# Matrix products that take turns over PSUM banks: three loop orders changed in a one-core encoder block

## The chip, the core and the metric

The kernel runs on one core of one Trainium2 chip. The metric is the device time of one execution in microseconds (us). Before the change three runs took 2044.85, 2045.12 and 2049.2 us, median 2045.12. The engines are named as in the profile: PE is TensorE's products, PEld its weight loads, DVE is VectorE, ACT is ScalarE, POOL is GpSimd, SP is SyncE, which here issues DMAs.

## What is computed

One layer of an encoder block for 256 tokens of width 2048, in float32. Cut to what matters here:

```python
h = rms_norm(x, norm1_g)
z = h @ w_in                       # columns: attention q, k, v, gates; recurrence q, f, i, gate; two merge gates
ya = forgetting_attention(...) @ w_a_up
yb = gated_recurrence(...) @ w_b_up
x = x + (sigmoid(ga) * ya + sigmoid(gb) * yb) @ w_o
h2 = rms_norm(x, norm2_g)
q = h2 @ peer_wq                   # product keys: 16 of 128 x 128 experts for each token and head
x = x + sum over chosen experts of gate * gelu(h2 . U[expert]) * V[expert]
out = rms_norm(x, norm_f_g)
```

## The kernel before

Each float32 operand of a large product is split into a high and a low part of the type fp32r, and a product of two matrices is made of three: high by high, high by low, low by high, all added up in PSUM.

**Projections.** Weights come in 38 groups of 512 columns. A group is worked off in units of four 128-row blocks (`UK = 4`) of the contraction, four units to a group, or two where the contraction is 1024 long. For a unit SP loads 1 MB into `raw`, ACT writes its high part to `w_hi` (L606), DVE the low part to `w_lo` (L951), and PE waits once, for `lo_ready`, and then runs the unit's products into `acc`. `w_hi` and `w_lo` have two buffers each, so the next unit is split while PE works. `acc[128, 2, 1024]` is PSUM: group `g` uses the half `g % 2`, which is two banks of 512 float32 columns, and the other half is emptied meanwhile. The last product of a unit signals `unit_done`.

- A *transposed unit* (L1698 to L1701) has the weights stationary and 256 tokens moving. Its four feature blocks of 128 each take 256 columns: features 0 and 1 lie in the first bank, 2 and 3 in the second. There are 48 such units, of 4 x 4 x 3 = 48 products.
- A *natural unit* (L1715 to L1717) has a token tile of 128 stationary and 512 weight columns moving. Token tile 0 fills the first bank and tile 1 the second. There are 88 such units, of 4 x 2 x 3 = 24 products.

In both, the three products of one feature or one token tile follow each other.

**Middle.** The gather of expert rows and their dot products, and the scatter of the experts' weights, keep DVE, ACT, POOL and the DMA queues busy. PE has little to do there, and the change doesn't touch that code.

**Dense value stage.** The last 1344 columns of the value table are not gathered: for each of 128 blocks of 128 experts the whole block is loaded (`v_raw`, three buffers, SP), split by ACT into `v_hi` (L887) and by DVE into `v_lo` (L1637), and multiplied by the 128 x 128 weights of the block's experts (`e_hi`, `e_lo`) for each of two token tiles. One block for one token tile is a *pass* of nine products (L2021 to L2023): the 1344 columns are three pieces of 512, 512 and 320 (`VBANKS`), each in a bank of its own, in `acc` for token tile 0 and in `scr` for token tile 1, and each piece has three products. The last product of a pass signals `v_used`, on which ACT's and DVE's next write to these buffers waits. Beside this, POOL gathers the first 704 columns of the chosen rows (L560) and DVE adds them up (L1620).

What sets the order on PE is the program's text: each engine runs its own instructions as written, and semaphores hold them together. The loops of the three functions below are thus the order of the products.

Of the kernel before, what the change touches and what calls it, by code (L numbers as in the profile page):

```python
# [11 lines left out]
P = 128  # L12
S = 256
NT = S // P
# [4 lines left out]
GW = 512  # L19
FB = GW // P  # L20
# [12 lines left out]
UK = 4  # L33


def units_of(g):

    narrow = G_AUP <= g < G_GB or (G_GB <= g < G_WO and (g - G_GB) % 2)
    return (HW if narrow else D) // P // UK
# [17 lines left out]
BLOCKS = P  # L57
# [144 lines left out]
def build(nc, x, norm1_g, w_in, fox_f_bias, hg_lb_logits, hg_norm_g, w_a_up, w_b_up, w_o, norm2_g,  # L202
# [16 lines left out]
    with ctx:  # L219
# [26 lines left out]
        def at(name, kib, shape, dt=fp32):  # L246
            return nc.alloc_sbuf_tensor_at(name, [P, *shape], dt, offset=arena_at + int(kib * 1024))
# [5 lines left out]
        w_hi = at("w_hi", 64, [2, UK, GW], f32r)  # L253
        w_lo = at("w_lo", 80, [2, UK, GW], f32r)
# [22 lines left out]
        v_hi = at("v_hi", 184, [2, DW], f32r)  # L277
# [64 lines left out]
        acc = ctx.enter_context(nc.psum_tensor("acc", [P, 2, 2 * GW], fp32))  # L342
# [1326 lines left out]
        def _(pe):  # L1669
            t_ = nc.tensor  # L1670
# [12 lines left out]
            def transposed_unit(g, m, src, i=0, per=0):  # L1683

                pe.wait_ge(lo_ready, UNIT0[g] + m + 1 + i * per)
                if m == 0:

                    pe.wait_ge(acc_free[g % 2], 1 + g // 2 + i)
                hi_, lo_ = src
                end = m == units_of(g) - 1  # L1690
                for k in range(UK):
                    kk = m * UK + k
                    for f in range(FB):
                        to, cols = acc[:, g % 2, f * S:(f + 1) * S], slice(f * P, (f + 1) * P)
                        wh, wl = w_hi[:, m % 2, k, cols], w_lo[:, m % 2, k, cols]
                        last_k = end and k == UK - 1

                        t_.matmul(to, wh, hi_[:, kk, :], start=kk == 0 and f % 2 == 0, stop=False,  # L1698
                                  skip_group_check=True)
                        t_.matmul(to, wh, lo_[:, kk, :], start=False, stop=False, skip_group_check=True)  # L1700
                        last = t_.matmul(to, wl, hi_[:, kk, :], start=False, stop=last_k, skip_group_check=True)  # L1701
                last.then_inc(unit_done, 1)

            def natural_unit(g, m, src, i=0, per=0):

                pe.wait_ge(lo_ready, UNIT0[g] + m + 1 + i * per)
                if m == 0:
                    pe.wait_ge(acc_free[g % 2], 1 + g // 2 + i)
                hi_, lo_ = src
                end = m == units_of(g) - 1  # L1710
                for k in range(UK):
                    kk = m * UK + k
                    for t in range(NT):
                        to, cols = acc[:, g % 2, t * GW:(t + 1) * GW], slice(t * P, (t + 1) * P)
                        t_.matmul(to, hi_[:, kk, cols], w_hi[:, m % 2, k, :], start=kk == 0, stop=False)  # L1715
                        t_.matmul(to, hi_[:, kk, cols], w_lo[:, m % 2, k, :], start=False, stop=False)  # L1716
                        last = t_.matmul(to, lo_[:, kk, cols], w_hi[:, m % 2, k, :], start=False,  # L1717
                                         stop=end and k == UK - 1)
                last.then_inc(unit_done, 1)

# [25 lines left out]
            for n in range(4):  # L1746
                pe.wait_ge(normed, 2 + n // 2 * 2)
                transpose_norm(f"h{n}", n)
                if n:
                    pe.wait_ge(h_ready, n)  # L1750
                    transposed_unit(G_HQF, n - 1, hT)
            pe.wait_ge(h_ready, 4)
            transposed_unit(G_HQF, 3, hT)
            for g in range(G_HQF + 1, G_HIG):
                for m in range(4):
                    transposed_unit(g, m, hT)
            loop_two(G_HIG, natural_unit, hT)

            def level_products(name, a, b, side, pieces):
# [12 lines left out]
            for n in range(4):  # L1772
                g = G_FQK + n
                for m in range(4):
                    transposed_unit(g, m, hT)
                    if m % 2:
                        lv = 2 * n + m // 2
                        pe.wait_ge(level_ready, lv + 1)
                        e = level[lv % 2]
# [8 lines left out]
            to = scr[0:H, half, 0:S]  # L1788
            for k in range(KD):
                t_.matmul(to, wff_hi[:, k, :], hT_hi[:, k, :], start=k == 0, stop=False)  # L1790
                t_.matmul(to, wff_lo[:, k, :], hT_hi[:, k, :], start=False, stop=False)
                last = t_.matmul(to, wff_hi[:, k, :], hT_lo[:, k, :], start=False, stop=k == KD - 1)
            done("forget", last)

            natural_unit(G_FV, 0, hT)
            natural_unit(G_FV, 1, hT)
            natural_unit(G_FV, 2, hT)
            natural_unit(G_FV, 3, hT)
# [6 lines left out]
            for t in range(NT):  # L1805
                last = t_.transpose(scr[:, half, t * H:(t + 1) * H], ff[:, 1, t * P:(t + 1) * P], ident[0:H, 0:H])
# [56 lines left out]
            for n in range(4):  # L1863
                g = G_GA + n
# [26 lines left out]
            for n in range(4):  # L1891
                g = G_GB + 2 * n
                for m in range(4):
# [4 lines left out]
                    if n == 0 and m == 1:  # L1898
                        pe.wait_ge(ob_ready, 1)
                        for t in (1, 0):  # L1900
                            half = enter(f"ob{t}")
                            for h in range(H):
                                last = t_.transpose(scr[:, half, h * P:(h + 1) * P], o_hg[:, t, h * P:(h + 1) * P],
                                                    ident[:, :])
# [7 lines left out]
                if n < 2:  # L1912
                    pe.wait_ge(keys_in, 16)
                    half = enter(f"keys{n}")
                    for u in range(8):
                        last = t_.transpose(scr[:, half, u * P:(u + 1) * P], keys_sb[:, 8 * n + u, :], ident[:, :])
# [6 lines left out]
            for g in range(G_WO + 1, G_WQ):  # L1923
                for m in range(4):
                    natural_unit(g, m, hT)
                    if m == 2:
                        n = g - G_WO - 1
# [14 lines left out]
            for n in range(4):  # L1942
                g = G_WQ + n
# [67 lines left out]
            for n in range(BLOCKS):  # L2011
                e_cols = slice(n % 2 * P, (n % 2 + 1) * P)
                def add(t, pieces, low):

                    pe.wait_ge(e_ready, n // 2 * 2 + t + 1)
                    flat = (acc, scr)[t][:, :, :].rearrange("p a n -> p (a n)")
                    eh, el = e_hi[:, n // 2 % 2, t, e_cols], e_lo[:, n // 2 % 2, t, e_cols]
                    for at0, end in pieces:
                        to, cols = flat[:, at0:end], slice(at0, end)
                        stop = n == BLOCKS - 1  # L2020
                        t_.matmul(to, eh, v_hi[:, n % 2, cols], start=False, stop=False, skip_group_check=True)  # L2021
                        t_.matmul(to, eh, low[:, cols], start=False, stop=False, skip_group_check=True)  # L2022
                        last = t_.matmul(to, el, v_hi[:, n % 2, cols], start=False, stop=stop, skip_group_check=True)  # L2023
                    return last

                pe.wait_ge(v_ready, 2 * n + 2)
                for t in range(NT):
                    add(t, VBANKS, v_lo[n % 2]).then_inc(v_used, 1)
# [24 lines left out]
```

## Time and profile before

| | |
|---|---|
| median of three runs | 2045.12 us (2044.85 to 2049.2) |
| span of the profiled execution | 2047.2 us; the page gives no other time for it |
| PE busy | 1436.2 us, 70%, 7933 products |
| PEld busy | 1248.8 us, 7933 weight loads |
| DVE busy | 1608.7 us, 79% |
| ACT, POOL busy | 868.3 us, 42%; 994.3 us, 49% |
| mean granted PE clock | 0.841 of full |

The page cuts the span into 40 slices of about 51 us. Products on PE overlap: one lasts longer in the rows than the distance to the next one's start, and PE's throughput is read from the starts. PE's busy share is an average over stages that differ.

### The profile page before, as it was taken

How to read it: one execution, taken by the hardware profiler on the slowest of the kernel's cores; microseconds unless marked ns; L12 is line 12 of the kernel's file. 1: busy time of each engine (PE TensorE's matmuls, PEld its weight loads, DVE VectorE, ACT ScalarE, POOL GpSimd, SP SyncE). 2: the span in 40 equal slices, each digit the busy share in tenths (PEclk: the TensorE clock that was granted, in tenths of full speed). 3: DMA queues.
4: the chain of work that ended last, by engine and by line, in shares of the span. 5: the costliest groups of instructions: out<-in, count | busy, mean ns of one | idle time of the engine just before them, and what ended most of it. 6: DMA issues, size and time to landing. Idle time of an engine off the chain costs nothing.

```text
span 2047.2 us, 22565 instructions
## 1 busy us (share of the span) xinstructions
PE 1436.2 (70%) x7933; PEld 1248.8 (61%) x7933; DVE 1608.7 (79%) x1995; ACT 868.3 (42%) x1130; POOL 994.3 (49%) x699
## 2 busy tenths in 40 slices
PE   6999999999999999920000002212359999999997
PEld 6987998877888789920000001111247888888886
DVE  5465775454755556789999999977889999999998
ACT  4353443344343444311211226567856444444444
POOL 1002320000000000178888888888888788888862
PEclk9999999999999999965555555555569999999999
DMA  5555434444555555789999999999965999999996
GB/s 207 185 185 185 157 132 144 142 156 155 195 184 185 187 184 176 277 346 407 418 417 415 419 400 421 414 422 414 421 244 195 389 386 390 398 406 390 390 384 235
DMA packets 151803, 601.81 MB, mean 294 GB/s; under 512 B 14720, under 2 KB 14736, under 8 KB 118288
## 3 DMA queue, kind: packets, MB, share of 16 engines
q0 software_dynamic: 58048, 364.41, 44.0%
q1 hardware_dynamic: 93648, 236.02, 32.2%
q8 instruction: 61, 1.00, 0.2%
q14 instruction: 46, 0.38, 0.0%
HBM read 598.29 MB, written 2.10 MB: 293 GB/s over the span
## 4 chain that ended last, share of the span: by engine, by line
PE 55%; DVE 16%; issue 14%; POOL 7%; DMA 6%; ACT 2%; DVEq 0%; POOLq 0%; SPq 0%; ACTq 0%
PE acc L1715 7%; PE acc L1716 7%; PE acc L1717 7%; DVE slots L1470 6%; POOL slots L537 5%; PE acc L1698 4%; PE acc L1700 4%; PE acc L1701 4%; PE acc L2021 3%; PE scr L2022 3%; PE acc L2022 3%; DMA v_raw<-in_v_dense 3%; PE scr L2021 3%; PE scr L2023 3%; PE acc L2023 3%
## 5 line engine op out<-in xcount | busy, mean ns | idle before, releaser
L951 DVE TENSOR_TENSOR w_lo<-raw,w_hi 128x2048 fp32r<-128x2048 f32 x136 | 314.6, 2314 | 281.8 <-ACT w_hi L606 280.7
L1470 DVE SCALAR_TENSOR_TENSOR slots<-slots,acc 128x2048 f32<-128x2048 f32 x188 | 424.6, 2284 | 44.0 <-DMA slots<-in_peer_u,expert 41.7
L606 ACT ACTIVATE w_hi<-raw 128x2048 fp32r<-128x2048 f32 x136 | 260.1, 1913 | 409.0 <-PE acc L1717 263.3
L560 POOL DMA_INDIRECT starts<-in_v_gather,expert x256 | 365.1, 1426 | 92.9 <-DVE X L1620 77.7
L537 POOL DMA_INDIRECT slots<-in_peer_u,expert x256 | 250.2, 977 | 241.9 <-DVE expert L1442 145.2
L545 POOL TENSOR_TENSOR slots<-slots,N 128x2048 f32<-128x2048 f32 x62 | 280.5, 4524 | 37.2 <-DMA slots<-in_peer_u,expert 37.1
L887 ACT ACTIVATE v_hi<-v_raw 128x1344 fp32r<-128x1344 f32 x128 | 170.5, 1332 | 260.5 <-PE scr L2023 202.7
L800 ACT ACTIVATE slots<-slots 128x2048 f32<-128x2048 f32 x62 | 118.4, 1909 | 341.2 <-POOL slots L545 341.2
L1978 PE MATMUL scr<-hot_a,hot_b 128*128 128x128 f32 x448 | 92.4, 372 | 222.1 <-DVE hot_b L1515 158.4
L1620 DVE SCALAR_TENSOR_TENSOR X<-starts,weight,X 128x704 f32<-128x704 f32 x256 | 241.9, 945 | 0.7 <-DMA starts<-in_v_gather,expert 0.3
L1715 PE MATMUL acc<-w_hi,hT_hi 128*128 128x512 f32 x576 | 227.9, 396 | 2.5 <-DVE w_lo L951 2.5
L1716 PE MATMUL acc<-w_lo,hT_hi 128*128 128x512 f32 x576 | 225.5, 391 | 0.0
L1717 PE MATMUL acc<-w_hi,hT_lo 128*128 128x512 f32 x576 | 225.3, 391 | 0.0
L1978 PEld LDWEIGHTS scr<-hot_a,hot_b 128*128 128x128 f32 x448 | 80.2, 269 | 235.4 <-issue 196.7
L1637 DVE TENSOR_TENSOR v_lo<-v_raw,v_hi 128x1344 fp32r<-128x1344 f32 x128 | 199.3, 1557 | 9.9 <-issue 8.0
L1698 PE MATMUL acc<-hT_hi,w_hi 128*128 128x256 f32 x512 | 146.7, 287 | 0.7 <-DVE hT_lo L976 0.7
L1700 PE MATMUL acc<-hT_lo,w_hi 128*128 128x256 f32 x512 | 145.7, 285 | 0.0
L1701 PE MATMUL acc<-hT_hi,w_lo 128*128 128x256 f32 x512 | 145.7, 285 | 0.0
L2021 PE MATMUL acc<-v_hi,e_hi 128*128 128x512 f32 (+1 forms) x384 | 141.3, 368 | 3.6 <-DVE v_lo L1637 2.7
L510 POOL TENSOR_TENSOR T<-T 128x1024 f32<-128x1024 f32 x8 | 20.0, 2494 | 250.9 <-DVE T L1084 148.1
L2022 PE MATMUL scr<-v_lo,e_hi 128*128 128x512 f32 (+1 forms) x384 | 140.5, 366 | 0.0
L2022 PE MATMUL acc<-v_lo,e_hi 128*128 128x512 f32 (+1 forms) x384 | 140.5, 366 | 0.0
(297 smaller groups left out, 3224.1 us busy)
## 6 DMA issues: line engine op xcount, KB each, us to landing
raw<-in_w_in SPq DMA_DIRECT2D x88, 1024.0 KB, 4.9
v_raw<-in_v_dense SPq DMA_DIRECT2D x128, 672.0 KB, 7.4
raw<-in_w_o SPq DMA_DIRECT2D x16, 1024.0 KB, 5.1
raw<-in_peer_wq SPq DMA_DIRECT2D x16, 1024.0 KB, 5.2
raw<-in_w_a_up SPq DMA_DIRECT2D x8, 1024.0 KB, 5.0
raw<-in_w_b_up SPq DMA_DIRECT2D x8, 1024.0 KB, 5.1
slots<-in_peer_u,expert POOLq DMA_INDIRECT x256, 9.6
starts<-in_v_gather,expert POOLq DMA_INDIRECT x256, 8.0
```

What stands on the lines that cost most here:

```text
L537: pool.indirect_dma_start(slots[j][:, :], None, u_rows, bass.IndirectOffsetOnAxis(ap=expert[:, t, k:k + 1], axis=0)).then_inc(row_landed[j ...
L545: g.tensor_tensor(slots[j][:, :], slots[j][:, :], N1[:, q // NSEL, :], ALU.mult).then_inc(product_ready, 1)
L560: pool.indirect_dma_start(starts[j][:, :], None, v_gather[:, :], bass.IndirectOffsetOnAxis(ap=expert[:, s // NSEL, s % NSEL:s % NSEL + 1], ...
L606: a.activation(w_hi[:, m % 2, :, :], raw[:, m % 2, :, :], ACT.Copy).then_inc(hi_ready, 1)
L951: v.tensor_tensor(w_lo[:, m % 2, :, :], raw[:, m % 2, :, :], w_hi[:, m % 2, :, :].bitcast(fp32), ALU.subtract).then_inc(lo_ready, 1)
L1470: v.scalar_tensor_tensor(out=slots[j][:, :], in0=slots[j][:, :], scalar=1.0, in1=row, op0=ALU.mult, op1=ALU.mult, accum_out=hid_sum[:, t, ...
L1620: v.scalar_tensor_tensor(out=X[:, t, 0:CW], in0=starts[start_at(s)][:, :], scalar=weight[:, t, k:k + 1], in1=X[:, t, 0:CW], op0=ALU.mult, ...
L1715: t_.matmul(to, hi_[:, kk, cols], w_hi[:, m % 2, k, :], start=kk == 0, stop=False)
L1716: t_.matmul(to, hi_[:, kk, cols], w_lo[:, m % 2, k, :], start=False, stop=False)
L1717: last = t_.matmul(to, lo_[:, kk, cols], w_hi[:, m % 2, k, :], start=False, stop=end and k == UK - 1)
L2021: t_.matmul(to, eh, v_hi[:, n % 2, cols], start=False, stop=False, skip_group_check=True)
L2022: t_.matmul(to, eh, low[:, cols], start=False, stop=False, skip_group_check=True)
```

## The change

Within a unit or a pass the same products run, on the same operands, into the same columns, in another order. In a transposed unit the features go in the pairs (0, 2) and (1, 3), one of each bank, and the three products are made pair by pair. In a natural unit the two token tiles take turns within each of the three products. In a dense pass the three pieces take turns within each of the three products. Flags that start and stop an accumulation go with their product. ACT, DVE and SP have the same instructions in the same order as before.

```diff
                     kk = m * UK + k
-                    for f in range(FB):
-                        to, cols = acc[:, g % 2, f * S:(f + 1) * S], slice(f * P, (f + 1) * P)
-                        wh, wl = w_hi[:, m % 2, k, cols], w_lo[:, m % 2, k, cols]
-                        last_k = end and k == UK - 1
-
-                        t_.matmul(to, wh, hi_[:, kk, :], start=kk == 0 and f % 2 == 0, stop=False,
-                                  skip_group_check=True)
-                        t_.matmul(to, wh, lo_[:, kk, :], start=False, stop=False, skip_group_check=True)
-                        last = t_.matmul(to, wl, hi_[:, kk, :], start=False, stop=last_k, skip_group_check=True)
+                    last_k = end and k == UK - 1
+                    for pair in ((0, 2), (1, 3)):
+                        to = [acc[:, g % 2, f * S:(f + 1) * S] for f in pair]
+                        wh, wl = ([w[:, m % 2, k, f * P:(f + 1) * P] for f in pair] for w in (w_hi, w_lo))
+                        for b in range(2):
+                            t_.matmul(to[b], wh[b], hi_[:, kk, :], start=kk == 0 and pair[b] % 2 == 0, stop=False,
+                                      skip_group_check=True)
+                        for b in range(2):
+                            t_.matmul(to[b], wh[b], lo_[:, kk, :], start=False, stop=False, skip_group_check=True)
+                        for b in range(2):
+                            last = t_.matmul(to[b], wl[b], hi_[:, kk, :], start=False, stop=last_k,
+                                             skip_group_check=True)
...
                     kk = m * UK + k
+                    to = [acc[:, g % 2, t * GW:(t + 1) * GW] for t in range(NT)]
+                    hi_k, lo_k = ([a[:, kk, t * P:(t + 1) * P] for t in range(NT)] for a in (hi_, lo_))
                     for t in range(NT):
-                        to, cols = acc[:, g % 2, t * GW:(t + 1) * GW], slice(t * P, (t + 1) * P)
-                        t_.matmul(to, hi_[:, kk, cols], w_hi[:, m % 2, k, :], start=kk == 0, stop=False)
-                        t_.matmul(to, hi_[:, kk, cols], w_lo[:, m % 2, k, :], start=False, stop=False)
-                        last = t_.matmul(to, lo_[:, kk, cols], w_hi[:, m % 2, k, :], start=False,
+                        t_.matmul(to[t], hi_k[t], w_hi[:, m % 2, k, :], start=kk == 0, stop=False)
+                    for t in range(NT):
+                        t_.matmul(to[t], hi_k[t], w_lo[:, m % 2, k, :], start=False, stop=False)
+                    for t in range(NT):
+                        last = t_.matmul(to[t], lo_k[t], w_hi[:, m % 2, k, :], start=False,
                                          stop=end and k == UK - 1)
...
-                    for at0, end in pieces:
-                        to, cols = flat[:, at0:end], slice(at0, end)
-                        stop = n == BLOCKS - 1
-                        t_.matmul(to, eh, v_hi[:, n % 2, cols], start=False, stop=False, skip_group_check=True)
-                        t_.matmul(to, eh, low[:, cols], start=False, stop=False, skip_group_check=True)
-                        last = t_.matmul(to, el, v_hi[:, n % 2, cols], start=False, stop=stop, skip_group_check=True)
+                    for e, v, stop in ((eh, v_hi[:, n % 2, :], False), (eh, low[:, :], False),
+                                       (el, v_hi[:, n % 2, :], n == BLOCKS - 1)):
+                        for at0, end in pieces:
+                            last = t_.matmul(flat[:, at0:end], e, v[:, at0:end], start=False, stop=stop,
+                                             skip_group_check=True)
```

PE, one block of the contraction in a natural unit, before (`acc` is written, the weights move, a part of the normed tokens is stationary; the size is the product's output):

```order
L1715 MATMUL acc<-w_hi,hT_hi 128x512
L1716 MATMUL acc<-w_lo,hT_hi 128x512
L1717 MATMUL acc<-w_hi,hT_lo 128x512
L1715 MATMUL acc<-w_hi,hT_hi 128x512
L1716 MATMUL acc<-w_lo,hT_hi 128x512
L1717 MATMUL acc<-w_hi,hT_lo 128x512
```

The same place on PE after the change, two blocks of the contraction (x2 is two equal rows in a row, here token tile 0 and token tile 1):

```order
L1719 MATMUL acc<-w_hi,hT_hi 128x512 x2
L1721 MATMUL acc<-w_lo,hT_hi 128x512 x2
L1723 MATMUL acc<-w_hi,hT_lo 128x512 x2
L1719 MATMUL acc<-w_hi,hT_hi 128x512 x2
L1721 MATMUL acc<-w_lo,hT_hi 128x512 x2
L1723 MATMUL acc<-w_hi,hT_lo 128x512 x2
```

Before, six rows are one block of the contraction, and the bank changes after each third product; after, it changes at every product.

PE, the first dense pass, before (`acc` is written, `v_hi` or `v_lo` moves, `e_hi` or `e_lo` is stationary):

```order
L2021 MATMUL acc<-v_hi,e_hi 128x512
L2022 MATMUL acc<-v_lo_90,e_hi 128x512
L2023 MATMUL acc<-v_hi,e_lo 128x512
L2021 MATMUL acc<-v_hi,e_hi 128x512
L2022 MATMUL acc<-v_lo_90,e_hi 128x512
L2023 MATMUL acc<-v_hi,e_lo 128x512
L2021 MATMUL acc<-v_hi,e_hi 128x320
L2022 MATMUL acc<-v_lo_90,e_hi 128x320
L2023 MATMUL acc<-v_hi,e_lo 128x320
```

The same pass on PE after the change:

```order
L2027 MATMUL acc<-v_hi,e_hi 128x512 x2
L2027 MATMUL acc<-v_hi,e_hi 128x320
L2027 MATMUL acc<-v_lo_90,e_hi 128x512 x2
L2027 MATMUL acc<-v_lo_90,e_hi 128x320
L2027 MATMUL acc<-v_hi,e_lo 128x512 x2
L2027 MATMUL acc<-v_hi,e_lo 128x320
```

The widths of the nine products were six times 512 and then three times 320; they are now 512, 512, 320, three times over.

## Rows read from the trace of the kernel before

**Rows 1.** The page's slices: busy tenths of TensorE, and its granted clock.

```profile
PE   6999999999999999920000002212359999999997
PEclk9999999999999999965555555555569999999999
```

**Rows 2.** Stages: length; busy us of five engines; PEclk, DMA share, GB/s.

```profile
60.00:218.00 158.00, 155.52 (x947) 138.93 (x946) 87.73 (x51) 69.66 (x40) 11.48 (x4) 1.00 0.53 183
390.50:392.20 1.70, 1.70 (x5) 1.32 (x4) 1.11 (x1) 0.00 (x0) 0.00 (x0) 0.50 0.30 117
530.00:690.00 160.00, 159.11 (x728) 131.56 (x728) 90.24 (x54) 63.48 (x39) 0.00 (x0) 1.00 0.54 184
1700.00:1850.00 150.00, 147.61 (x724) 125.30 (x722) 144.77 (x163) 66.48 (x83) 123.81 (x88) 1.00 1.01 398
1850.00:2000.00 150.00, 149.58 (x739) 127.92 (x738) 147.84 (x165) 66.76 (x83) 117.01 (x84) 1.00 1.01 388
```

**Rows 3.** Timeline, transposed units: start us, us, engine, line, operation; first and last product.

```profile
19.62 0.58 PE L1698 MATMUL acc<-hT_hi,w_hi 128*128 128x256 f32 x1 [0.73 <-DVE hT_lo L976]
...
75.81 0.28 PE L1701 MATMUL acc<-hT_hi,w_lo 128*128 128x256 f32 x1
75.93 0.28 PE L1698 MATMUL acc<-hT_hi,w_hi 128*128 128x256 f32 x1
76.05 0.28 PE L1700 MATMUL acc<-hT_lo,w_hi 128*128 128x256 f32 x1
76.17 0.28 PE L1701 MATMUL acc<-hT_hi,w_lo 128*128 128x256 f32 x1
76.29 0.28 PE L1698 MATMUL acc<-hT_hi,w_hi 128*128 128x256 f32 x1
...
880.29 0.28 PE L1701 MATMUL acc<-h2T_hi,w_lo 128*128 128x256 f32 x1
```

**Rows 4.** Timeline, natural units: first products, one unit's, and the last.

```profile
115.53 0.40 PE L1715 MATMUL acc<-w_hi,hT_hi 128*128 128x512 f32 x1
...
116.00 0.39 PE L1717 MATMUL acc<-w_hi,hT_lo 128*128 128x512 f32 x1
...
116.92 0.39 PE L1715 MATMUL acc<-w_hi,hT_hi 128*128 128x512 f32 x1
...
432.23 0.39 PE L1715 MATMUL acc<-w_hi,hT_hi 128*128 128x512 f32 x1
432.46 0.39 PE L1716 MATMUL acc<-w_lo,hT_hi 128*128 128x512 f32 x1
432.69 0.39 PE L1717 MATMUL acc<-w_hi,hT_lo 128*128 128x512 f32 x1
432.91 0.39 PE L1715 MATMUL acc<-w_hi,hT_hi 128*128 128x512 f32 x1
...
435.63 0.39 PE L1715 MATMUL acc<-w_hi,hT_hi 128*128 128x512 f32 x1
...
777.75 0.39 PE L1717 MATMUL acc<-w_hi,hT_lo 128*128 128x512 f32 x1
```

**Rows 5.** Timeline, dense stage: first products of two passes, six passes apart.

```profile
2019.39 0.39 PE L2021 MATMUL scr<-v_hi,e_hi 128*128 128x512 f32 x1
...
2030.31 0.39 PE L2021 MATMUL scr<-v_hi,e_hi 128*128 128x512 f32 x1
```

**Rows 6.** Waits, 1545 to 2047 us: who waited for whom; us, times, longest us.

```profile
ACT v_hi L887 <- PE scr L2023: 202.7, 100, 4.0
...
ACT v_hi L887 <- DMA v_raw<-in_v_dense: 57.1, 26, 3.3
...
PE acc L2021 <- DVE v_lo L1637: 2.7, 6, 0.8
```

**Rows 7.** Timeline, a natural unit at 391 us.

```profile
391.00 0.63 PE L1717 MATMUL acc<-w_hi,hT_lo 128*128 128x512 f32 x1
391.43 0.63 PE L1715 MATMUL acc<-w_hi,hT_hi 128*128 128x512 f32 x1
```

## The prediction, made before the changed kernel was run

> **What bounds the kernel now.** I read the page's slices first, then the table by stage, then the starts of single TensorE products. In the slices the reader is to see two long stretches in which TensorE is busy nine tenths or more, the projections (to about 880 us) and the dense value stage (from 1564 us), with a middle in which it is nearly idle [rows 1]; only the two outer stretches issue the products that the change reorders. The table by stage confirms it: 155.52 of 158 us and 159.11 of 160 us in two stretches of the projections, 147.61 and 149.58 of 150 us in two of the dense stage, all at a granted clock of 1.00 [rows 2]. In the projections TensorE alone is that full (VectorE 87.73 of 158, DMA share 0.53), so any nanosecond per product there goes straight to the end. In the dense stage VectorE (147.84 of 150) and the DMA share (1.01) are as full as TensorE [rows 2], so a gain there would soon meet another limit, a loss would not.
>
> The mean duration of a product says nothing here, since products overlap; the distance from one start to the next is the cost. In the transposed units (two 256-wide features to a bank) the starts stand 0.12 us apart [rows 3], in the natural units (one 512-wide token tile to a bank) 0.227: 15 products from 432.23 to 435.63 [rows 4], 3.40/15. The difference, 0.1067 us for 256 columns, is 0.417 ns a column, one per cycle of the upper level (2.4 GHz). What is left is a fixed 13.3 ns a product at either width. If the change can win anything in the projections, it wins it from these 13.3 ns.
>
> **The change part by part.** It adds and removes no instruction: 2304 transposed products (48 units of 48), 2112 natural (88 of 24), 2304 dense (256 passes of 9), before and after. ScalarE, VectorE and SyncE run the same rows in the same order, each unit's or pass's last product still carries the semaphore, and every wait stands ahead of the unit, so no wait is added or taken.
>
> 1. *Transposed units.* Of 12 consecutive products 2 now step to another bank; after, all 12 do. The rows of before already hold every case. From 75.81 (feature 1, bank 0) to 75.93 (feature 2, bank 1) the bank changes; 75.93 to 76.05 and 76.17 accumulates onto the same columns; 76.17 to 76.29 is the same bank, other columns. All are 0.12 us [rows 3]. Over all 48 units (the first and the last row of that line are shown [rows 3]) the median distance at each of the 12 places of a step is 120 ns, those with a bank change and those without. Price of a step within a bank over a step to another: 0.
> 2. *Natural units.* 2 of 6 steps change the bank now, all 6 after. 432.69 to 432.91 changes it, 432.23 to 432.46 and to 432.69 does not: 0.22, 0.23, 0.23 us [rows 4], and over the 88 units (first and last row shown) the median at each of the six places is 227 ns. Price 0.
>  The two other things that the order changes are seen too. Consecutive products on one stationary operand (432.23, 432.46) and on a new one (432.69) cost the same, as do those with the same moving operand (432.69, 432.91). So the sum for 4416 products is 0. Its bounds: 3328 steps change their kind (10/12 of 2304 = 1920, 4/6 of 2112 = 1408); the medians resolve 1 ns, so at most 3.3 us either way.
> 3. *Dense stage.* Six passes of 9 products run from 2019.39 to 2030.31 [rows 5]: 1.820 us a pass. With the settled prices, 6 x 0.2267 + 3 x 0.1467 (320 columns at 0.417 ns and 13.3 ns) = 1.800, so 20 ns a pass are extra. They can't be the bank's, since natural units have the same steps and lack them. Rows 4 show something alike: when widths change from 256 to 512 at 115.53, six products take 1.39 us instead of 1.36 and then settle, 17 ns of the 30 within the first two (115.53 to 116.00: 0.47 instead of 0.453). A pass now has one such change (three 320 wide, then six 512 wide); after, the pieces take turns 512, 512, 320 and a pass has three changes.
>  Lower bound: the 20 ns vanish, 256 x 20 = -5.1 us. Upper: each change costs the whole 20, 60 a pass instead of 20, +10.2 us. I take the value between that the row at 115.53 gives: only two 512-wide products follow each change, so about half the settling is paid, 3 x 10 = 30 ns a pass, +10 ns, +2.6 us. TensorE was idle for 2.39 and 0.42 us in two thirds of the stage [rows 2], waiting for v_lo (6 waits, 2.7 us [rows 6]); a TensorE that runs a little longer per block waits less there, so I count +1.
>
> Sum: 0 + 0 + 1. The profiled execution has a span of 2047.2 us, 2.1 above the median of the runs, 2045.12, and inside their spread (2044.85 to 2049.2); the page gives no time around the span. On the median: 2046 us. What hides nothing: if point 1 or 2 is wrong, no engine covers it.
>
> The fixed 13.3 ns may be weighed against a rule. The Trainium skill (TensorE: Matmul & The Clock Gate, Back-to-back issue gap) puts an isolated product at its columns per 2.4 GHz and 2.5 ns; by it the 4416 projection products would be about 11 ns shorter each, 48 us in all, if the reorder brought them there. The trace does not give that price at a step to another bank either.
>
> **Rivals.**
>
> *A. The fixed 13.3 ns is the turnaround of a bank.* Then the 3328 projection steps that change their kind give back 13.3 ns each, 44 us, and 6 x 256 dense steps some 20 us more, of which the full DMA queues leave little: about 2000 us. For it: the 13.3 ns are there at both widths. Against it: they are also there at each step that changes the bank today [rows 3, 4]. 0.03.
>
> *B. The dense passes lose their extra.* With all 20 ns gone and nothing else in the way, 2045.1 - 5.1 = 2040. For it: the extra is there only in that stage. Against it: three width changes in place of one, and DMA and VectorE as full as TensorE; ScalarE already waited 26 times for v_raw's DMA (57.1 us) beside 100 times for TensorE [rows 6]. With half of it eaten it is no change that can be told. 0.07 for a gain over the bound below.
>
> *C. Slower: width changes.* Place: the dense passes; price: 20 ns for each change of width, three in place of one; it decides from about +16 ns a pass on (4.1 us over 256 passes). At the full price +10.2, less up to 3 us of idle that it fills: 2052 to 2055. For it: rows 4 and the 20 ns. Against it: a pair of 512-wide products does not live long enough to pay the whole settling. 0.17.
>
> *D. Slower: the clock.* From 390.5 to 392.2 us the granted clock was 0.50, the lower level of 1.2 GHz [rows 2], and 512-wide products stood 0.43 us apart [rows 7] instead of 0.227. If bank turns made the clock fall for a tenth of the 2112, that is 211 x 0.2 = 42 us, about 2088. For it: nothing in the rows; the new order gives TensorE no new reason to wait, and 1.00 stood through stretches that changed bank every third product [rows 2].
> The Trainium skill has a rule of this kind (TensorE: Matmul & The Clock Gate, A second HAM failure mode: psum-queue depth-cycling): a kernel that cycled through banks each iteration idled in between and its clock swung. By it the sum would be the 2088 of rival D. The trace disagrees so far: its stretches with bank steps show no idle and no swing. 0.02.
>
> *E. The order is changed but no price depends on it:* 2045, my forecast without the +1; it shares the forecast's chance.
>
> **How the numbers follow.** About 0.2% (4.1 us) is what a measurement of this kernel tells from no change. Forecast and E: 0.71, own range 2042 to 2050 (the bounds of points 1 and 2 and the spread of the runs). Faster: A 0.03, B 0.07, and 0.02 that the forecast's own spread falls past the bound, 0.12. Slower: C, mostly past the bound, 0.14; D 0.02; 0.02 of the forecast's spread: 0.18; the milder part of C, 0.03, joins no change: 0.70. The range takes in B at 2040 and C up to 2054 and leaves A, D and the edge of C out.
>
> **What would show it.** Right: starts 0.12 us apart in the transposed units and 0.227 in the natural ones, dense passes between 1.82 and 1.84 us, the granted clock at 1.00 in the same stretches. Starts of about 0.11 and 0.215 us prove A and the forecast wrong; a pass of 1.80 with the stage shorter proves B; a pass of 1.85 or more with the 512s after a 320 stretched proves C; 0.43 us with a clock of 0.5 proves D. What would surprise the whole argument is a price of the order that no step of before shows, such as steps that return to a bank after exactly one product elsewhere, a case which the trace lacks.

## The result, and the profile after

The changed kernel takes 2053.79 us (median of 11 runs, 2051.8 to 2060.83), the kernel before in the same comparison 2048.12 us (11 runs, 2044.27 to 2054.14): ratio of the runs 1.0034, 95% interval 1.0023 to 1.0044, about 7 us slower (the two medians lie 5.7 us apart). The forecast was +1 us, which can't be told from no change. What happened is rival C, at the size that it gave as its full price.

The table by stage of the changed kernel (columns as in [rows 2]):

```profile
60.00:218.00 158.00, 155.51 (x947) 138.93 (x946) 86.78 (x52) 70.72 (x40) 11.48 (x4) 1.00 0.55 181
...
1700.00:1850.00 150.00, 149.79 (x722) 126.19 (x722) 145.07 (x162) 66.38 (x83) 124.10 (x87) 1.00 1.01 396
1850.00:2000.00 150.00, 149.83 (x724) 126.54 (x724) 144.92 (x161) 65.91 (x82) 122.55 (x82) 1.00 1.00 380
```

The stretch of the projections holds as many products (x947) and as many busy microseconds as before. In the dense stage TensorE is now busy to 149.79 and 149.83 of 150 us (147.61 and 149.58 before [rows 2]) and yet it starts fewer products (722 instead of 724, and 724 instead of 739 from 1850 us on). From 1850 us on VectorE's share falls from 147.84 to 144.92 and the moved data from 388 to 380 GB/s; in the stretch before they hardly move. TensorE became fuller and finished less: it got slower there. The clock stayed at 1.00.

The timeline of the changed kernel shows the same by single products (start us, us, what; equal products that follow each other are merged, and x3 with 128x512 in its name is two 512 wide and one 320 wide). First the projections, a transposed and a natural stretch; then the dense stage, one pass and a bit, and the starts of two passes five apart:

```profile
75.48 0.40 PE L1698 MATMUL acc<-hT_hi,w_hi 128*128 128x256 f32 x2
75.72 0.40 PE L1701 MATMUL acc<-hT_lo,w_hi 128*128 128x256 f32 x2
...
76.20 0.40 PE L1698 MATMUL acc<-hT_hi,w_hi 128*128 128x256 f32 x2
...
451.58 0.62 PE L1719 MATMUL acc<-w_hi,hT_hi 128*128 128x512 f32 x2
...
454.30 0.62 PE L1719 MATMUL acc<-w_hi,hT_hi 128*128 128x512 f32 x2
...
1897.70 0.78 PE L2027 MATMUL acc<-v_hi,e_hi 128*128 128x512 f32 x3
1898.32 0.78 PE L2027 MATMUL acc<-v_lo,e_hi 128*128 128x512 f32 x3
1898.94 0.78 PE L2027 MATMUL acc<-v_hi,e_lo 128*128 128x512 f32 x3
1899.56 0.63 PE L2027 MATMUL scr<-v_hi,e_hi 128*128 128x512 f32 x2
...
2024.82 0.78 PE L2027 MATMUL acc<-v_hi,e_hi 128*128 128x512 f32 x3
...
2034.12 0.40 PE L2027 MATMUL scr<-v_hi,e_hi 128*128 128x512 f32 x1
```

Six transposed products from 75.48 to 76.20 are 0.72 us, 0.12 each, as in [rows 3]. Twelve natural products from 451.58 to 454.30 are 2.72 us, 0.2267 each, as in [rows 4]. So a bank change at every step costs and brings nothing there. In the dense stage each triple of 512, 512 and 320 takes 0.62 us where its settled prices make 0.600, and a pass takes 1.860 us (9.30/5) where [rows 5] have 1.820. Over the whole stage 237 of the 255 distances from one pass to the next are within 6 ns of 1.860, as 228 were of 1.820 before; most of the others hold a wait or follow one. That is 40 ns a pass and 256 x 40 ns = 10.2 us of TensorE.

Not all of it reaches the end. Waits after (us, times, longest us):

```profile
ACT v_hi L887 <- PE scr L2027: 220.9, 105, 4.0
...
ACT v_hi L887 <- DMA v_raw<-in_v_dense: 45.6, 21, 2.8
...
PE acc L2027 <- DVE v_lo L1637: 0.3, 1, 0.3
```

TensorE waits 0.3 us for v_lo instead of 2.7, and ScalarE waits more for TensorE and less for v_raw's DMA than in [rows 6]. Counted over all passes as start distances above the settled pass, TensorE's idle time in the stage fell from 5.9 to 2.5 us. 10.2 - 3.4 = 6.8 us is the lengthening of the stage, from 471.6 to 478.5 us between its first and its last start, and agrees with the ratio. It is one trace against one: the two experiments below that have one half of the change each give 474.9 us with the old dense loop and 480.2 us with the new one.

### The profile page after: what moved, and what is told of

Its sections match the earlier page's. It is cut to its first block, busy times and chain, and to the rows that moved or that the text cites. A ratio compares the mean times of both kernels' runs of the same rounds, so it can differ in the third digit from the quotient of the medians.

```text
span 2051.1 us, 22565 instructions
## 1 busy us (share of the span) xinstructions
PE 1443.8 (70%) x7933; PEld 1250.6 (61%) x7933; DVE 1609.8 (78%) x1995; ACT 868.0 (42%) x1130; POOL 995.1 (49%) x699
## 4 chain that ended last, share of the span: by engine, by line
PE 57%; DVE 15%; issue 14%; POOL 7%; DMA 5%; ACT 2%; DVEq 0%; POOLq 0%; SPq 0%; ACTq 0%
PE acc L2027 10%; PE scr L2027 10%; PE acc L1719 7%; PE acc L1721 7%; PE acc L1723 7%; DVE slots L1470 6%; POOL slots L537 6%; PE acc L1698 4%; PE acc L1703 4%; PE acc L1701 4%; DMA slots<-in_peer_u,expert 2%; DMA v_raw<-in_v_dense 2%; DVE w_lo L951 2%; PE scr L1770 1%; DVE hot_b L1521 1%
## 5 line engine op out<-in xcount | busy, mean ns | idle before, releaser
L1719 PE MATMUL acc<-w_hi,hT_hi 128*128 128x512 f32 x576 | 180.9, 395 | 2.5 <-DVE w_lo L951 2.5
L1721 PE MATMUL acc<-w_lo,hT_hi 128*128 128x512 f32 x576 | 178.8, 392 | 0.0
L1723 PE MATMUL acc<-w_hi,hT_lo 128*128 128x512 f32 x576 | 178.4, 391 | 0.0
L1723 PEld LDWEIGHTS acc<-w_hi,hT_lo 128*128 128x128 f32 x576 | 109.0, 189 | 23.1
L1719 PEld LDWEIGHTS acc<-w_hi,hT_hi 128*128 128x128 f32 x576 | 106.8, 189 | 26.7 <-DVE w_lo L951 6.0
L1721 PEld LDWEIGHTS acc<-w_lo,hT_hi 128*128 128x128 f32 x576 | 108.7, 189 | 23.1
L1698 PE MATMUL acc<-hT_hi,w_hi 128*128 128x256 f32 x512 | 104.0, 285 | 0.7 <-DVE hT_lo L976 0.7
```

The costliest lines, as they stand in the source:

```text
L1719: t_.matmul(to[t], hi_k[t], w_hi[:, m % 2, k, :], start=kk == 0, stop=False)
L1721: t_.matmul(to[t], hi_k[t], w_lo[:, m % 2, k, :], start=False, stop=False)
L1723: last = t_.matmul(to[t], lo_k[t], w_hi[:, m % 2, k, :], start=False, stop=end and k == UK - 1)
```

## The experiments

**The two halves of the change.** The projections alone, as a diff from the changed kernel, whose dense loop goes back:

```diff
-                    for e, v, stop in ((eh, v_hi[:, n % 2, :], False), (eh, low[:, :], False),
-                                       (el, v_hi[:, n % 2, :], n == BLOCKS - 1)):
-                        for at0, end in pieces:
...
+                    for at0, end in pieces:
+                        to, cols = flat[:, at0:end], slice(at0, end)
...
```

> Only the transposed and natural units have the new order; the dense passes are as before. Theory (the price is one of width changes within the dense passes): no change, ratio 1.000 within 0.001; products 120 and 227 ns apart, dense pass 1.820 us. Rival (a step to another bank at every product costs something somewhere in the projections too): part of the 7 us shows here, ratio 1.001 to 1.003, with distances above 120 or 227 ns.

Measured: 2048.2 us against 2048.41, ratio 1.0000 (0.9990 to 1.0010). The reverse, only the dense loop changed (this and all further diffs start from the kernel before):

```diff
-                    for at0, end in pieces:
-                        to, cols = flat[:, at0:end], slice(at0, end)
...
+                    for e, v, stop in ((eh, v_hi[:, n % 2, :], False), (eh, low[:, :], False),
+                                       (el, v_hi[:, n % 2, :], n == BLOCKS - 1)):
+                        for at0, end in pieces:
```

> Only the dense passes have the new order. Theory (width changes): the whole loss is here, dense pass 1.860 us, +40 ns x 256 = 10.2 us on TensorE, of which about 3 us disappear in its former idle time: ratio 1.0025 to 1.0045. Rival (projections): ratio below 1.002.

Measured: 2054.04 us, ratio 1.0028 (1.0017 to 1.0040), pass 1.860 us. The whole loss is the dense loop's.

Its trace shows one thing more, near the start of the stage:

```profile
1570.12 0.77 PE L2021 MATMUL scr<-v_hi,e_hi 128*128 128x512 f32 x3
...
1577.40 0.40 PE L2021 MATMUL scr<-v_hi,e_hi 128*128 128x512 f32 x1
...
1579.62 0.87 PE L2021 MATMUL acc<-v_hi,e_hi 128*128 128x512 f32 x3 [0.23 <-DVE v_lo L1637]
...
1583.40 0.78 PE L2021 MATMUL acc<-v_hi,e_hi 128*128 128x512 f32 x3
...
1585.26 0.40 PE L2021 MATMUL scr<-v_hi,e_hi 128*128 128x512 f32 x1
```

Four passes from 1570.12 take 1.820 us each (7.28/4), in the new order of widths; after the wait for v_lo at 1579.62 the same order takes 1.860, as from 1583.40 on. The granted clock is 1.00 in both stretches. Of the passes of this run five are at the low price, 232 at the high one. So the new order makes 1.860 the usual price, but the widths alone do not fix it.

**Bank steps or widths.** The 512-wide pieces take turns, the 320-wide one follows:

```diff
-                    for at0, end in pieces:
...
+                    for same in (pieces[0:2], pieces[2:3]):
+                        for e, v, stop in terms:
+                            for at0, end in same:
```

> Dense passes in which the two 512-wide pieces take turns over their banks (six products), and then the 320-wide piece has its three products; projections as before. 7 of 9 steps go to another bank (before 3, after 9), but the width changes as often as before. Theory (width changes): pass 1.820 us, ratio 1.000 within 0.001. Rival (bank steps cost): six more changed steps cost 40 ns in the new order, so four more cost about 27 here: pass 1.845 us or more, ratio about 1.002.

Measured: 2047.98 us, ratio 0.9999 (0.9990 to 1.0008). Its timeline, one pass:

```profile
1897.05 0.63 PE L2023 MATMUL acc<-v_hi,e_hi 128*128 128x512 f32 x2
1897.52 0.62 PE L2023 MATMUL acc<-v_lo,e_hi 128*128 128x512 f32 x2
1897.98 0.62 PE L2023 MATMUL acc<-v_hi,e_lo 128*128 128x512 f32 x2
1898.44 0.30 PE L2023 MATMUL acc<-v_hi,e_hi 128*128 128x320 f32 x1
...
1898.87 0.63 PE L2023 MATMUL scr<-v_hi,e_hi 128*128 128x512 f32 x2
```

1.82 us a pass with 7 of 9 steps to another bank. The reverse mix keeps the changed kernel's sequence of widths but puts some products on the same columns one after the other (p is the piece, k which of its three products):

```diff
+                    for p, k in ((0, 0), (0, 1), (2, 0), (0, 2), (1, 0), (2, 1), (1, 1), (1, 2), (2, 2)):
+                        (at0, end), (e, v, ends) = pieces[p], terms[k]
...
```

> A dense pass whose products are interleaved so that the widths run 512, 512, 320 three times over, as in the changed kernel, but with 2 of the 9 steps accumulating onto the same bank and columns as the product before (7 go to another bank, as in the run with the 320-wide products together, whose pass took 1.820 us); projections as before. Theory (the sequence of widths sets the price, the banks do not): pass 1.860 us. Rival (the loss needs every step to go to another bank): pass between 1.820 and 1.850 us.

```profile
1907.02 0.40 PE L2022 MATMUL acc<-v_hi,e_hi 128*128 128x512 f32 x1
1907.26 0.40 PE L2022 MATMUL acc<-v_lo,e_hi 128*128 128x512 f32 x1
1907.49 0.31 PE L2022 MATMUL acc<-v_hi,e_hi 128*128 128x320 f32 x1
1907.64 0.40 PE L2022 MATMUL acc<-v_hi,e_lo 128*128 128x512 f32 x1
...
1908.88 0.40 PE L2022 MATMUL scr<-v_hi,e_hi 128*128 128x512 f32 x1
```

Again 1.86 us a pass (one run took 2054.64 us, before beside it 2044.84), with the same number of steps to another bank as the kernel that took 1.82. These two runs tell banks and widths apart: it is the interleaving of the widths that brings the 1.86, and the number of steps to another bank does not.

**Fewer changes of width.** Token tile 1 takes the pieces backwards:

```diff
-                    for at0, end in pieces:
+                    for at0, end in (pieces if t == 0 else pieces[::-1]):
```

> The order of before, but token tile 1 goes through the pieces backwards (320, 512, 512), so that two passes have one stretch of 320-wide and one of 512-wide products: half as many width changes. Bank steps as before. Theory (20 ns for each return to 512): two passes 3.620 us instead of 3.640, -2.6 us on TensorE, of which the full DMA and VectorE may leave little: ratio 0.998 to 1.000. Rival (320-wide products cost 6.7 ns more each, whatever stands beside them, and the new order costs by its bank steps): two passes 3.640 us, ratio 1.000.

```profile
1891.26 0.39 PE L2021 MATMUL acc<-v_hi,e_hi 128*128 128x512 f32 x1
...
1892.62 0.30 PE L2021 MATMUL acc<-v_hi,e_hi 128*128 128x320 f32 x1
...
1893.50 0.39 PE L2021 MATMUL scr<-v_hi,e_hi 128*128 128x512 f32 x1
...
1894.88 0.39 PE L2021 MATMUL acc<-v_hi,e_hi 128*128 128x512 f32 x1
```

Two passes take 3.62 us instead of 3.64, as the theory said. The time does not follow clear of the noise: 2046.79 us, ratio 1.0001 (0.9988 to 1.0014), where the whole 2.6 us would be 0.9987.

**Is each return worth 20 ns?** Two returns to 512 in a pass:

```diff
+                    for p, k in ((0, 0), (0, 1), (0, 2), (2, 0), (1, 0), (1, 1), (1, 2), (2, 1), (2, 2)):
...
```

> A dense pass with two returns to 512: widths 512, 512, 512, 320, 512, 512, 512, 320, 320; five of nine steps go to another bank. Theory (20 ns for each return): pass 1.840 us. Rival (the price depends on how many 320-wide products stand alone, or settles only in regular triples): another value between 1.810 and 1.860 us.

```profile
1893.96 0.39 PE L2022 MATMUL acc<-v_hi,e_hi 128*128 128x512 f32 x1
...
1894.66 0.53 PE L2022 MATMUL acc<-v_hi,e_hi 128*128 128x320 f32 x2
1895.03 0.40 PE L2022 MATMUL acc<-v_lo,e_hi 128*128 128x512 f32 x1
...
1895.79 0.39 PE L2022 MATMUL scr<-v_hi,e_hi 128*128 128x512 f32 x1
```

1.820 us a pass in some stretches and 1.826 to 1.827 in others (2048.65 us in one run), not 1.840. (Four of the nine steps go to another bank, not five as the expectation has it.) So the price is no fixed 20 ns a return: two returns lose 20 to 27 ns over the settled prices, three returns to pairs of 512s lose 60. Threes of 512-wide products lose less than pairs, though pairs have less time to settle in.

**No changes of width at all.** Three pieces of 448 columns, each at the start of its own bank, in the old order and in the new one:

```diff
-VBANKS = ((0, 512), (512, 1024), (1024, DW))
+VW = DW // 3
...
+VBANKS = ((0, VW), (VW, 2 * VW), (2 * VW, DW))
...
-                        to, cols = flat[:, at0:end], slice(at0, end)
+                        to, cols = banked(flat, at0, end), slice(at0, end)
```

> The 1344 dense columns in three pieces of 448 in place of 512, 512, 320, each still at the start of its own bank; order of before (three products of a piece in a row). The reads at the end go over the three pieces. Theory (width changes): no width changes are left, so a pass costs 9 x (448 x 0.417 + 13.3) = 1.800 us, 20 ns less than before, -5.1 us on TensorE, part of which DMA and VectorE may take back: ratio 0.997 to 0.9995. Rival (the 20 ns belong to the dense stage itself, its buffers or its DMA traffic): pass 1.820 us, ratio 1.000.

> Three pieces of 448 as in the run before it, in the changed kernel's order: every step goes to another bank, and no width changes. Theory: a step to another bank costs nothing, pass 1.800 us as with the old order, ratio 0.997 to 0.9995. Rival (bank steps cost 40 ns a pass in the changed kernel): pass 1.84 us, ratio 1.001 to 1.004.

Measured: 2051.35 us, ratio 1.0014 (1.0003 to 1.0024), and 2052.44 us, ratio 1.0022 (1.0011 to 1.0033), before being 2047.93. Two passes of the second one:

```profile
1942.65 0.77 PE L2039 MATMUL acc<-v_hi,e_hi 128*128 128x448 f32 x3
...
1944.48 0.77 PE L2039 MATMUL scr<-v_hi,e_hi 128*128 128x448 f32 x3
...
1946.30 0.36 PE L2039 MATMUL acc<-v_hi,e_hi 128*128 128x448 f32 x1
```

In both most passes take about 1.824 us (3.648 for these two). The banks make no difference here either, which the second run was for. But the theory missed: 1.800 was expected. A 448-wide product costs 202.7 ns in these passes where the line through 256 and 512 gives 200.0; the distances go 199, 207, 203, 202, 202 and round again. And there is a second price. In the first of the two kernels, four passes:

```profile
1776.16 0.37 PE L2039 MATMUL scr<-v_hi,e_hi 128*128 128x448 f32 x1
...
1783.60 0.37 PE L2039 MATMUL scr<-v_hi,e_hi 128*128 128x448 f32 x1
```

They take 1.860 us each (7.44/4), every step 206 or 207 ns, at a granted clock of 1.00 like the others. Such stretches begin after a pause of TensorE and mostly last to the next one; 67 of the 255 passes of the first kernel and 52 of the second are of this kind. With the 4 ns of the other passes they make about 3 us in each profiled execution, most or all of the loss. So one and the same sequence, without any change of width, has two prices, and it mostly goes from one to the other where TensorE starts anew.

Four more kernels look at other widths. Pieces of 320 alone, and of 384 alone (shown is the first; the other has (0, 384) and (512, 896)):

```diff
-                    add(t, VBANKS, v_lo[n % 2]).then_inc(v_used, 1)
+                    add(t, ((0, 320), (512, 832), (1024, 1344)), v_lo[n % 2]).then_inc(v_used, 1)
```

> Dense passes of three pieces of 320 columns each (384 of the 1344 columns are left out), order of before, so that no width changes within the stage. Theory (only a return to a wider product costs): 9 x 146.7 = 1.320 us a pass. Rival (320 is an awkward width in itself, as 448 turned out to be, 202.7 ns where the line through 256 and 512 gives 200.0): 150 to 153 ns a product, 1.350 to 1.380 us.

> Dense passes of two pieces of 384 columns (576 are left out), six products, no change of width. The line through 256 and 512 gives 173.3 ns a product, 1.040 us a pass. Theory (only changes of width cost): 1.040. Rival (widths other than 256 and 512 have a price of their own, as 448 has): 175 to 180 ns a product, 1.050 to 1.080 us.

The kernel with 320 alone, a pass that follows another without a wait, and a stretch of its stage table:

```profile
1765.16 0.31 PE L2021 MATMUL scr<-v_hi,e_hi 128*128 128x320 f32 x1
...
1766.33 0.31 PE L2023 MATMUL scr<-v_hi,e_lo 128*128 128x320 f32 x1
```

```profile
1700.00:1850.00 150.00, 118.48 (x736) 107.70 (x735) 145.86 (x164) 67.01 (x85) 123.19 (x90) 1.00 1.02 401
```

Eight steps take 1.17 us, 146 ns each, and the median of the whole stage is 147: on the line, so 320 is not dear in itself. The stage table says something else as well. TensorE is busy for only 118.48 of 150 us, and the kernel's one run took 2047.43 us, no less than before. As far as one run shows, the stage was already nearly as long as VectorE (145.86) and the DMA (1.02) make it: from its first to its last start it takes 470.5 us, 471.6 before, and 463.7 with 384 alone. For 384 the commonest distances are 173 and 174 ns, on the line too, but TensorE waits so often in that kernel (2041.41 us) that whole passes can't be compared; that run is inconclusive.

The changed order with a narrower third piece (the dense loop of the run with the dense half alone, and this):

```diff
-                    add(t, VBANKS, v_lo[n % 2]).then_inc(v_used, 1)
+                    add(t, VBANKS[0:2] + ((1024, 1280),), v_lo[n % 2]).then_inc(v_used, 1)
```

(For 128 columns the last pair is (1024, 1152).)

> The changed kernel's dense order with pieces of 512, 512 and 256 columns (64 columns are left out, to see what a change of width costs at another width); projections as before. The settled prices give 6 x 226.7 + 3 x 120 = 1.720 us. If each return to 512 costs a fixed 20 ns: pass 1.780 us. If the price grows with the difference of the widths (20 ns for 192 columns): 26.7 ns each, 1.800 us.

> The same with pieces of 512, 512 and 128 columns (192 are left out). Products 128 wide stand 112 ns apart in the trace of before; the settled prices give 6 x 226.7 + 3 x 112 = 1.696 us. Fixed 20 ns: 1.756 us. By the difference of the widths (40 ns each): 1.816 us.

Measured: 2040.66 and 2040.86 us in one run each. TensorE waits for v_lo in many passes, so only single triples can be read. With 256 the median triple is 587 ns, 13.7 above its settled 573.3, but most spread from 572 to 595; with 128 most lie between 569 and 592 ns, against 565.3, with no common value. Neither the fixed 20 ns nor a price that grows with the difference of the widths fits. (The 112 ns in the 565.3 come from other 128-wide products; here a lone one stands 59 ns before the next, and the 512 after it about 285 before its own successor.)

These two kernels, which leave out columns, lie below all 20 runs of before beside them (median 2047.93, the lowest 2043.37). With 256 the median distance from pass to pass is 1.764 us, 56 ns or in all 14 us less of TensorE, and about 7 us came of it.

No experiment that does all the work beats the kernel before beyond its interval. The mirrored order has the shortest pass of the kernels that do all the work, and the time stays.

## Why the prediction was wrong

- *What bounds the kernel*: right for the dense stage, where a gain meets another limit and a loss does not. The mirrored order (10 ns a pass less) and the all-320 kernel (TensorE busy a fifth less in the stretch shown, one run) gained nothing that could be told, and the third piece of 256 about half of what TensorE saved (one run); 40 ns a pass more cost 7 us of 10. That the projections' products go straight to the end was not put to the test, since their price did not change.
- *Steps 1 and 2, the projections at 0*: right. The rows of before held every kind of step that these prices need, and the new ones cost 0.12 and 0.2267 us. The projections alone gave a ratio of 1.0000.
- *Step 3, the dense passes*: wrong in the size, and this is the step that failed. It was to be "+10 ns" a pass, because "only two 512-wide products follow each change, so about half the settling is paid". It is +40 ns, the upper bound that the step itself gave. The inference from the start of a natural unit at 115.53 [rows 4] looked at the wide products alone. In the changed pass the two wide ones stand 235 and 233 ns before their successors, 14.7 over the settled price, near the 17 that the inference used; but the lone 320-wide one stands 152 ns before the next, 5 over, where the three 320-wide ones of the old pass were 143, 145 and 147, together 5 under. The old pass gives some of the settling back in its narrow stretch, and the new one pays there too. Nor is the settling at 115.53 special to a change of width. In the kernel before, a natural unit that follows another one and begins after a wait, with 512s on both sides, pays the same:

```profile
173.59 0.50 PE L1715 MATMUL acc<-w_hi,hT_hi 128*128 128x512 f32 x1 [0.89 <-DVE w_lo L951]
173.92 0.39 PE L1716 MATMUL acc<-w_lo,hT_hi 128*128 128x512 f32 x1
...
175.31 0.39 PE L1716 MATMUL acc<-w_lo,hT_hi 128*128 128x512 f32 x1
```

  Leaving out the first, six products take 1.39 us instead of 1.36, as at 115.53, and then the distances are 0.227. So both look like the run-in of a stream that starts anew, which the step took for a price of one transition. What it lacked is that a repeated pattern need not run in at all but can stay at a price of its own.
- *Hidden by idle time*: right in kind and near in size. "Up to 3 us" were to vanish in TensorE's idle time by rival C, and 3.4 did between the two traces. The size is rough: idle time was 5.9 and 9.1 us in the two traces with the old dense loop, 2.5 and 4.5 in the two with the new one.
- *Rivals*: C had the place and the size, and its upper case, 10.2 us less 3, is what came. Its rule, 20 ns for each change of width, fits the new and the mirrored order and fails for the others: two returns cost 20 to 27 ns, and 448s alone, without a change, 24 or 60. That it gave the right number for this order is in part luck. It got 0.17, and "does not live long enough to pay the whole settling" was the argument against it. That is refuted: over the settled prices the passes with two 512s to each 320 lose 60 ns, those with threes of 512s at most 27, and the old pass with its six 512s loses 20. A and D are refuted by the unchanged distances and clock of the projections, B by 1.860. (Against D the prediction said that stretches with bank steps show no idle; [rows 2] have 155.52 of 158 us, a little idle, and no swing of the clock.) The case named as a surprise, a return to a bank after exactly one product elsewhere, costs nothing (1.82 us with the 512-wide pieces taking turns).
- *The range*: 2053.79 lies just inside "C up to 2054", and that says little for the forecast. The range was drawn that far for rival C, and the runs of before in the comparison lie 3 us higher (2048.12) than the three that the sum started from. Against its own before the changed kernel lost about 7 us where +1 was forecast.

Open: why TensorE's handover takes longer in some sequences of widths, and why one sequence can run at either of two prices. The settled widths 256, 320 and 512 lie on one line, 448 lies 2.7 or 6.7 ns above it, and mixed sequences lie above it by amounts that neither the number of changes nor the difference of the widths explains. Nothing here shows what the product is waiting for.

## What to carry to other kernels

Before spreading products over PSUM banks, look for the steps of the present order that already change the bank: if they stand no further apart or closer than the others, expect nothing from the order of banks; here it gave nothing. Reordering can mix widths that stood together; keep products of one width in a row, and price a mixed pattern by running it, since its cost can't be read from one transition, and read more than one stretch of it, since the price can change at a wait. In the dense stage, where TensorE, VectorE and DMA are equally full, most of a few ns lost per product showed in the time, and of what was gained about half or less.

## What was not expected of the hardware

A product's price depends on its neighbours' widths even where TensorE never waits and its clock is full: a pass of six products of 512 and three of 320 columns took 1.81 us a pass in the mirrored order, 1.82 in the old one and mostly 1.86 in the new one. It depends on what went before as well. The new order ran at 1.82 for five passes and at 1.86 after a wait, and 448 columns alone cost 202.7 ns each in some stretches, with distances that cycle between 199 and 207, and a steady 206.7 in others, while 320 (147) and 512 (227) settle.
